# One core of a hybrid decoder layer: stationary expert weights for gate and up, 96 places an expert, buffers for 18 chunks, split distance 4

## The chip, the core and the metric

The kernel runs on one core of a Trainium2 chip. The core has a matrix engine (TensorE, PE in the rows), a vector engine (VectorE, DVE), a scalar engine (ScalarE, ACT), a general engine (GpSimd, POOL) and a queue for transfers (SyncE, SP), each with its own instruction stream, and 16 DMA engines that they share. The metric is the device time of one execution in microseconds (us), lower is better.

## The reference

One decoder layer over 512 tokens of width 1024, in float32. After a block of four token mixers comes a mixture of experts, and the change lies there alone:

```
def hier_moe(x, w_rg, b_rg, w_re, b_re, w_g, w_u, w_d):
    """Top-1 expert group, then top-2 experts inside it; SwiGLU experts."""
    ...
    for e in range(N_EXPERTS):
        h = jax.nn.silu(xt @ w_g[e]) * (xt @ w_u[e])
        out = out + gates[:, e:e + 1] * (h @ w_d[e]).astype(f32)
```

There are 16 experts with hidden width 512, and each of the 512 tokens goes to two of them, so an expert gets 64 tokens on average. `w_g` and `w_u` are 1024 by 512 an expert, `w_d` is 512 by 1024; all three are 100 MB together.

## The kernel before

Up to about 640 us the core computes the mixers. Then it routes: each token gets a place in the buffer of each of its two experts. If every expert has at most `CAP` = 128 tokens (`fits`, true for this input), the routed path runs, else a dense one that is not executed here.

**Chunks and steps.** The weights of an expert are six chunks of 1 MB: `g` 0 and 1, `u` 0 and 1, `d` 0 and 1. The table `STEPS` puts all 96 in one order: g, g, u, u of expert e, then d, d of expert e-1 (at the end: g14, d13, u14, g15, u15, d14, d15, two each). Chunk c is loaded by SP (`stage_load`, L445) into one of `NS` = 8 staging buffers. ACT writes its float16 upper half (`split`, L839), DVE the float16 lower half (`split`, L1726), into one of `NW` = 7 pairs of buffers. Then PE multiplies. A staging buffer is free when DVE has split it, and that lets SP issue the load of chunk c+8; a split buffer is free when PE has used it. ACT and DVE split chunk c+`LOOK` (6 ahead) at step c, before the other work of the step.

**A step on PE.** Every product is made of three (`products`, L963 to L965: upper by upper, upper by lower, lower by upper), each with its own load of the stationary operand. In all steps the tokens' activations are stationary (128 by 128) and the weights move, 512 columns at a time: 12 matmuls a step. Gate and up come out with a token in each row, so `h_transposes` (L1314) must turn the hidden values before the down step can use them.

**The chain of one expert.** POOL gathers its token rows (L566, two buffers `xg`). `x_transposes` on PE (L1306), placed behind u1 of the expert before, `x_hi` on ACT (L893, 2 of 512 columns) and `x_lo` on DVE (L1832, 2 of 512 columns) give `xgT`, held for two experts. After g1 ACT takes the tanh (L906), after u1 DVE makes the gated product (L1901, L1902), PE turns it, ACT and DVE halve it (L914, L1837; `H_AT` says at which steps), and PE uses it in the d steps. ACT copies the result out (L924) and POOL scatters it to rows in memory (L574). The last two experts are put back by matmuls (L1356) instead; the other rows are read back and added on DVE (`add_rows`, L1846, at four steps of `ROWS_AT`).

**Who waits for whom.** All queues run in order, so whatever stands behind a waiting instruction waits too. At u1 DVE does: split, `x_lo` of the next expert, gated product.

## Time and profile before

| | us |
|---|---|
| median of the runs | 971.64 |
| lowest | 970.34 |
| the profiled execution, its own time | 972.64 |
| its span in the trace | 970.7 |

So 1.94 us of the profiled execution lie around its span. The page gives busy time and share of the span:

```profile
PE 907.7 (94%) x5924; PEld 518.1 (53%) x5924; DVE 669.6 (69%) x877; ACT 491.5 (51%) x681; POOL 71.3 (7%) x89
L963 PE MATMUL bank<-arena 128*128 128x512 f16 (+1 forms) x1568 | 466.6, 318 | 16.4 <-DVE arena L1832 6.0
L1726 DVE SCALAR_TENSOR_TENSOR arena<-arena 128x2048 f16<-128x2048 f32 x96 | 217.1, 2286 | 42.6 <-ACT arena L839 42.6
L839 ACT ACTIVATE arena<-arena 128x2048 f16<-128x2048 f32 x96 | 181.5, 1908 | 24.8 <-PE bank L965 24.8
```

A group's row gives the line, the engine and the operation, what is written from what, the shape, the count, the busy time in us and the mean of one in ns, and then the idle time of the engine just before and what ended it. PE's busy time is of overlapping instructions; how long one takes of the engine is read from the distance between starts. PEld is the load of the stationary operand, which can run beside a matmul.

### The profile page before, as it was taken

How to read it: one execution, taken by the hardware profiler on the slowest of the kernel's cores; microseconds unless marked ns; L12 is line 12 of the kernel's file. 1: busy time of each engine (PE TensorE's matmuls, PEld its weight loads, DVE VectorE, ACT ScalarE, POOL GpSimd, SP SyncE). 2: the span in 40 equal slices, each digit the busy share in tenths (PEclk: the TensorE clock that was granted, in tenths of full speed). 3: DMA queues.
4: the chain of work that ended last, by engine and by line, in shares of the span. 5: the costliest groups of instructions: out<-in, count | busy, mean ns of one | idle time of the engine just before them, and what ended most of it. 6: DMA issues, size and time to landing. Idle time of an engine off the chain costs nothing.

```text
span 970.7 us, 14670 instructions
## 1 busy us (share of the span) xinstructions
PE 907.7 (94%) x5924; PEld 518.1 (53%) x5924; DVE 669.6 (69%) x877; ACT 491.5 (51%) x681; POOL 71.3 (7%) x89
## 2 busy tenths in 40 slices
PE   6999999999999998999999979928999999999884
PEld 4434784855766655444444449924455554545442
DVE  5677769541887775643344344557899999999887
ACT  5444373223454444233232324463787888888643
POOL 7000000003000000000000000010111211111000
PEclk9989999999999999999999989957999999999998
DMA  8702404527621102943443316255899999999742
GB/s 211 176 25 59 116 24 111 151 66 198 176 79 33 38 23 65 391 111 94 120 118 83 104 46 234 95 201 170 295 388 403 380 405 391 389 399 379 309 185 89
DMA packets 119454, 177.92 MB, mean 183 GB/s; under 512 B 14317, under 2 KB 99621, under 8 KB 107094
## 3 DMA queue, kind: packets, MB, share of 16 engines
q1 hardware_dynamic: 112176, 162.76, 48.8%
q0 software_dynamic: 6928, 13.61, 4.8%
q8 instruction: 49, 0.80, 0.3%
q10 hardware_dynamic: 278, 0.56, 0.2%
q14 instruction: 23, 0.19, 0.1%
HBM read 172.76 MB, written 16.22 MB: 195 GB/s over the span
## 4 chain that ended last, share of the span: by engine, by line
PE 88%; DVE 6%; ACT 3%; DMA 1%; issue 1%; DVEq 0%; ACTq 0%; POOLq 0%
PE bank L963 25%; PE bank L964 24%; PE bank L965 24%; PE bank L1176 3%; PE bank L1195 3%; PE bank L1306 2%; DVE arena L1726 1%; PE bank L1070 1%; PE bank L1185 1%; PE bank L1055 1%; ACT arena L839 1%; PE bank L1267 1%; PE bank L1314 1%; PE bank L1134 1%; DMA cst<-in_c_sq 1%
## 5 line engine op out<-in xcount | busy, mean ns | idle before, releaser
L963 PE MATMUL bank<-arena 128*128 128x512 f16 (+1 forms) x1568 | 466.6, 318 | 16.4 <-DVE arena L1832 6.0
L964 PE MATMUL bank<-arena 128*128 128x512 f16 (+1 forms) x1568 | 466.3, 318 | 0.0
L965 PE MATMUL bank<-arena 128*128 128x512 f16 (+1 forms) x1568 | 465.4, 317 | 0.0
L1726 DVE SCALAR_TENSOR_TENSOR arena<-arena 128x2048 f16<-128x2048 f32 x96 | 217.1, 2286 | 42.6 <-ACT arena L839 42.6
L963 PEld LDWEIGHTS bank<-arena 128*128 128x128 f16 x1568 | 155.7, 99 | 146.2 <-issue 36.5
L965 PEld LDWEIGHTS bank<-arena 128*128 128x128 f16 x1568 | 155.1, 99 | 112.6 <-issue 5.4
L964 PEld LDWEIGHTS bank<-arena 128*128 128x128 f16 x1568 | 154.9, 99 | 101.0 <-issue 4.9
L839 ACT ACTIVATE arena<-arena 128x2048 f16<-128x2048 f32 x96 | 181.5, 1908 | 24.8 <-PE bank L965 24.8
L606 ACT ACTIVATE arena<-arena 128x1024 f16<-128x1024 f32 (+1 forms) x92 | 92.5, 1007 | 101.9 <-PE bank L965 76.3
L1471 DVE SCALAR_TENSOR_TENSOR arena<-arena 128x1024 f16<-128x1024 f32 (+1 forms) x91 | 103.5, 1163 | 11.4 <-ACT arena L606 9.9
L660 ACT ACTIVATE arena<-bank 128x512 f32<-128x512 f32 x35 | 20.8, 595 | 92.3 <-PE bank L965 92.2
L780 ACT ACTIVATE arena<-arena,nmx 128x128 f32<-128x128 f32 (+3 forms) x48 | 26.9, 561 | 61.4 <-DVE nmx L1671 61.4
L1717 DVE SCALAR_TENSOR_TENSOR arena<-arena,bank 128x512 f32<-128x512 f32 x24 | 16.4, 685 | 57.7 <-PE bank L965 57.6
L830 ACT ACTIVATE arena<-bank,half 128x512 f32<-128x512 f32 x24 | 16.3, 679 | 49.8 <-PE bank L965 49.8
L1668 DVE TENSOR_TENSOR arena<-bank,arena 128x128 f32<-128x128 f32 (+3 forms) x48 | 23.5, 489 | 22.5 <-PE bank L1176 18.8
L1715 DVE SCALAR_TENSOR_TENSOR arena<-arena,bank 128x512 f32<-128x512 f32 x8 | 5.5, 687 | 48.1 <-PE bank L965 48.1
L1176 PE MATMUL bank<-arena 64*128 64x128 f32 (+3 forms) x96 | 38.6, 482 | 0.0
L1195 PE MATMUL bank<-arena 128*128 128x64 f32 x240 | 32.5, 267 | 1.2 <-ACT arena L789 1.1
L1195 PEld LDWEIGHTS bank<-arena 128*128 128x128 f32 x240 | 30.5, 191 | 3.0 <-ACT arena L789 2.2
L893 ACT ACTIVATE arena<-bank 128x512 f16<-128x512 f32 x32 | 17.5, 594 | 22.1 <-PE bank L1306 22.1
L574 POOL DMA_INDIRECT y_rows<-arena,row_of x14 | 21.9, 1561 | 92.1 <-ACT arena L924 92.1
L566 POOL DMA_INDIRECT arena<-x_rows,token_of x16 | 17.7, 1106 | 143.5 <-PE bank L1306 120.3
(275 smaller groups left out, 766.9 us busy)
## 6 DMA issues: line engine op xcount, KB each, us to landing
arena<-in_moe_wg SPq DMA_DIRECT2D x32, 1024.0 KB, 10.3
arena<-in_moe_wu SPq DMA_DIRECT2D x32, 1024.0 KB, 10.8
arena<-in_moe_wd SPq DMA_DIRECT2D x32, 1024.0 KB, 12.1
arena<-in_w_gate SPq DMA_DIRECT2D x32, 512.0 KB, 4.0
arena<-in_w_in SPq DMA_DIRECT2D x31, 512.0 KB, 3.9
arena<-in_w_branch SPq DMA_DIRECT2D x32, 192.0 KB, 3.6
y_rows<-in_c_tab SPq DMA_DIRECT2D x4, 1024.0 KB, 12.3
arena<-in_w_out SPq DMA_DIRECT2D x8, 512.0 KB, 5.0
```

Source lines behind the costliest of these rows:

```text
L574: pool.indirect_dma_start(out=y_rows, out_offset=bass.IndirectOffsetOnAxis(ap=row_of[:, e:e + 1], axis=0), in_=yout[e % 2], in_offset=None ...
L606: act.activation(*split_views(c, c_hi), ACT.Copy, scale=WSCALE).then_inc(S("c_hi_done"), 1)
L780: act.activation(pr[n % 3][:, 0:nk], lg[n % 3][:, 0:nk], ACT.Exp, bias=nmx[:, n % 4:n % 4 + 1], accum_out=lsum[:, (n // HEADS) % 2, n % HE ...
L839: act.activation(w_hi[c % NW], stage[c % NS], ACT.Copy, scale=WSCALE).then_inc(S("hi_done"), 1)
L963: pe.matmul(outb, lhs[0], rhs[0], start=first, stop=False, skip_group_check=True)
L964: pe.matmul(outb, lhs[0], rhs[1], start=False, stop=False, skip_group_check=True)
L965: return pe.matmul(outb, lhs[1], rhs[0], start=False, stop=last_, skip_group_check=True)
L1176: pe.matmul(lgb[n % 2][:, 0:(i + 1) * P], q[r, h // 2, i * P:(i + 1) * P], k[r, h // 2, 0:(i + 1) * P], start=True, stop=True).then_inc(S( ...
L1195: last = pe.matmul(ps[6 + g % 2][:, h * HD:(h + 1) * HD], pT[:, n % 2, b * P:(b + 1) * P], v[:, b, h * HD:(h + 1) * HD], start=(b == 0), s ...
L1471: ins = stt(lo, src, WSCALE, hi, ALU.mult, ALU.subtract)
L1668: sig("lg_read", tt(l, lgb[n % 2][:, 0:nk], bias[:, head, T - nk:T], ALU.add))
L1726: tell("split_done", stt(w_lo[c % NW], stage[c % NS], WSCALE, w_hi[c % NW], ALU.mult, ALU.subtract))
```

## The change

`CAP` falls from 128 to 96, `LOOK` from 6 to 4, the staging buffers go from 8 to 12 and the split pairs from 7 to 6 (together 18 chunks where there were 15). In the gate and up steps the weights become stationary, 128 hidden columns at a time, and the 96 token columns move: 48 matmuls a step. The hidden values then come out already turned, and `h_transposes`, `H_AT` and the buffers `hrow` go. The activations `xgT`, `sgr` and the gathered rows `xg` now have one buffer each where they had two. The d steps keep their 12 matmuls of 512 columns, with 96 stationary columns. Loads of d chunks take two rows of 4 KB for each partition where they took one run of 8 KB.

```
-CAP = P
+CAP = 96
-LOOK = 6
+LOOK = 4
...
+        STAGE = [17408, 24576, 29696, 44172, 46220, 26624, 33292, 35340, 4096, 6144, 10752, 15360]
+        SPLIT = [(40076, 41100), (42124, 43148), (37388, 38412), (0, 1024), (2048, 3072), (28672, 31744)]
+        EARLY, READY = 5, 10
+        SLOT = [*range(READY), *range(FIRST), READY, FIRST, READY + 1]
+        for _c in range(len(SLOT), len(STEPS)):
+            SLOT.append(SLOT[_c - NS])
...
-                for c in range(NS + FIRST, len(STEPS)):
-                    sp_.wait_ge(S("split_done"), c - NS + 1)
+                for c in range(READY + FIRST, len(STEPS)):
+                    if splits_ahead(c):
+                        sp_.wait_ge(S("split_done"), splits_ahead(c))
+                    elif c > READY + FIRST:
+                        sp_.wait_ge(S("x2_stored"), 16 * NT)
+                        sp_.wait_ge(S("token_full"), 2)
                     stage_load(c)
...
                 def x_hi(e):
                     for j in range(2):
                         act.wait_ge(S("xgT_full"), 2 * e + j + 1)
-                        if e >= 2:
-                            act.wait_ge(S("chunk_used"), steps_to("u", e - 2))
+                        if e >= 1:
+                            act.wait_ge(S("chunk_used"), steps_to("u", e - 1))
...
                         for k in range(4):
-                            last = products(bank[:, :], (hi[:, 4 * hf + k, :], lo[:, 4 * hf + k, :]),
-                                            (v[0][:, k, :], v[1][:, k, :]), hf == 0 and k == 0, hf == 1 and k == 3)
+                            for m in range(KH):
+                                last = products(bank[:, m * CAP:(m + 1) * CAP], [w[:, k, m * P:(m + 1) * P] for w in v],
+                                                (hi[:, 4 * hf + k, :], lo[:, 4 * hf + k, :]),
+                                                hf == 0 and k == 0 and m == 0, hf == 1 and k == 3)
...
-                    if (kind, e, hf) in H_AT:
-                        h_lo(H_AT[kind, e, hf])
+                    if STEPS[c - 1][0] == "u" and STEPS[c - 1][2]:
+                        h_lo(STEPS[c - 1][1])
...
-                    if c in ROWS_AT:
-                        add_rows(ROWS_AT[c])
...
+                    if c >= len(STEPS) - NT:
+                        add_rows(c - len(STEPS) + NT)
```

The order of the instructions changes at three places. The first is PE at the start of a g step in the middle of the expert phase; bank2 is the accumulator, and "waits" are the semaphores that the instruction waits for. Before, and then of the change:

```order
L963 MATMUL bank2<-arena 128x512 [waits split_done,h_ready,xlo_done]
L964 MATMUL bank2<-arena 128x512
L965 MATMUL bank2<-arena 128x512
L963 MATMUL bank2<-arena 128x512
L964 MATMUL bank2<-arena 128x512
L965 MATMUL bank2<-arena 128x512
```

```order
L977 MATMUL bank2<-arena 128x96 [waits split_done,h_ready,xlo_done]
L978 MATMUL bank2<-arena 128x96
L979 MATMUL bank2<-arena 128x96
L977 MATMUL bank2<-arena 128x96
L978 MATMUL bank2<-arena 128x96
L979 MATMUL bank2<-arena 128x96
```

The waits are the same; each matmul has 96 columns for 512, and there are 48 in the step for 12. The second place is DVE over the cycle of one expert. L1726 (now L1732) is the split of a chunk, L1832 (L1838) `x_lo`, L1901 and L1902 (L1899, L1900) the gated product, L1837 (L1843) `h_lo`. Before, and then of the change:

```order
L1726 SCALAR_TENSOR_TENSOR arena<-arena 128x2048 [waits hi_done]
L1832 TENSOR_TENSOR arena<-bank,arena 128x512 [waits xhi_done] x2
L1901 SCALAR_TENSOR_TENSOR arena<-arena,bank 128x512 [waits hgT_full,chunk_used,sgr_ready]
L1902 SCALAR_TENSOR_TENSOR arena<-arena,bank 128x512 [waits dve_step_routed]
L1726 SCALAR_TENSOR_TENSOR arena<-arena 128x2048 [waits hi_done] x5
L1837 TENSOR_TENSOR arena<-bank,arena 128x512 [waits hhi_done]
```

```order
L1838 TENSOR_TENSOR arena<-bank,arena 128x384 [waits xhi_done] x2
L1899 SCALAR_TENSOR_TENSOR arena<-arena,bank 128x384 [waits chunk_used,sg_ready]
L1900 SCALAR_TENSOR_TENSOR arena<-arena,bank 128x384 [waits dve_step_body]
L1732 SCALAR_TENSOR_TENSOR arena<-arena 128x2048 [waits hi_done]
L1843 TENSOR_TENSOR arena<-arena 128x384 [waits hhi_done]
L1732 SCALAR_TENSOR_TENSOR arena<-arena 128x2048 [waits hi_done] x5
```

Still six splits and five small operations, but the small ones have 384 columns, and `h_lo` stands one split behind the gated product and no longer five. The third place is DVE at the end, from the gated product of expert 15 on; L1846 (L1848) is `add_rows`, L1851 (L1853) the lower half of a result of the last two experts. Before, and then of the change:

```order
L1837 TENSOR_TENSOR arena<-bank,arena 128x512 [waits hhi_done]
L1846 SCALAR_TENSOR_TENSOR arena<-arena,wsel 128x1024 [waits tokens_in0]
L1846 SCALAR_TENSOR_TENSOR arena<-arena,wsel 128x1024 [waits dve_step_routed]
L1901 SCALAR_TENSOR_TENSOR arena<-arena,bank 128x512 [waits chunk_used,hgT_full,sgr_ready,dve_step_routed]
L1902 SCALAR_TENSOR_TENSOR arena<-arena,bank 128x512 [waits dve_step_routed]
L1846 SCALAR_TENSOR_TENSOR arena<-arena,wsel 128x1024 [waits tokens_in1]
```

```order
L1732 SCALAR_TENSOR_TENSOR arena<-arena 128x2048 [waits hi_done] x3
L1899 SCALAR_TENSOR_TENSOR arena<-arena,bank 128x384 [waits chunk_used,sg_ready]
L1900 SCALAR_TENSOR_TENSOR arena<-arena,bank 128x384 [waits dve_step_body]
L1843 TENSOR_TENSOR arena<-arena 128x384 [waits hhi_done]
L1848 SCALAR_TENSOR_TENSOR arena<-arena,wsel 128x1024 [waits tokens_in0]
L1848 SCALAR_TENSOR_TENSOR arena<-arena,wsel 128x1024 [waits dve_step_body]
```

Because splits now run 4 steps ahead, three of them stand between `h_lo` of expert 14 and the gated product of expert 15, and all four `add_rows` come behind that product, where the first came ahead of it.

## Rows read from the trace of the kernel before

**Rows 1.** Windows: span, PE, PEld, DVE, ACT, POOL busy; granted clock, DMA share, GB/s.

```profile
700.00:908.00 208.00, 208.00 (x1025) 104.16 (x1023) 201.34 (x136) 173.74 (x148) 30.85 (x24) 1.00 1.00 391
908.00:930.00 22.00, 16.97 (x76) 8.03 (x75) 16.17 (x11) 14.82 (x13) 2.16 (x2) 0.92 0.55 201
```

**Rows 2.** Chain that ended last: start, length, what; two x_transposes, 12 experts apart.

```profile
694.62 1.07 PE bank L1306 x8
...
899.50 1.06 PE bank L1306 x8
```

**Rows 3.** Timeline, DVE over one expert: start, length, operation, [idle before].

```profile
696.45 1.28 DVE L1832 TENSOR_TENSOR arena<-bank,arena 128x512 f16<-128x512 f32 x2
697.65 0.68 DVE L1901 SCALAR_TENSOR_TENSOR arena<-arena,bank 128x512 f32<-128x512 f32 x1
698.36 0.69 DVE L1902 SCALAR_TENSOR_TENSOR arena<-arena,bank 128x512 f32<-128x512 f32 x1
698.97 4.49 DVE L1726 SCALAR_TENSOR_TENSOR arena<-arena 128x2048 f16<-128x2048 f32 x2
703.82 4.49 DVE L1726 SCALAR_TENSOR_TENSOR arena<-arena 128x2048 f16<-128x2048 f32 x2 [0.37 <-ACT arena L839]
...
710.72 0.68 DVE L1837 TENSOR_TENSOR arena<-bank,arena 128x512 f16<-128x512 f32 x1
```

**Rows 4.** Timeline, ACT in the same expert.

```profile
701.87 3.71 ACT L839 ACTIVATE arena<-arena 128x2048 f16<-128x2048 f32 x2
...
712.31 1.08 ACT L893 ACTIVATE arena<-bank 128x512 f16<-128x512 f32 x2 [1.20 <-PE bank L1306]
```

**Rows 5.** Timeline, PE: two f16 matmuls of 512 columns, 12 apart.

```profile
780.91 0.38 PE L963 MATMUL bank<-arena 128*128 128x512 f16 x1
...
783.50 0.38 PE L963 MATMUL bank<-arena 128*128 128x512 f16 x1
```

**Rows 6.** Timeline, PE: two f16 matmuls of 128 columns, 20 apart.

```profile
629.91 0.22 PE L963 MATMUL bank<-arena 128*128 128x128 f16 x1
...
631.02 0.22 PE L965 MATMUL bank<-arena 128*128 128x128 f16 x1
```

**Rows 7.** Timeline, PEld: 10 f16 loads from neighbouring columns, before 16-column matmuls.

```profile
646.50 0.34 PEld L1274 LDWEIGHTS bank<-sel,cst 128*128 128x128 f16 x10 [4.15 <-DVE sel L1765]
```

**Rows 8.** Timeline, PE: 64 matmuls of 5 columns, stationary every 16th column.

```profile
668.19 4.07 PE L1293 MATMUL bank<-told,arena 128*128 128x5 f16 x64
```

**Rows 9.** DMA, 700 to 908 us: queue of SP; gathers, count, us to landing.

```profile
q1 hardware_dynamic: 10299, 74.95, 92.0%
...
arena<-x_rows,token_of POOLq DMA_INDIRECT x11, 8.4
```

**Rows 10.** DMA issues, 700 to 750 us: count, KB, us to landing.

```profile
arena<-in_moe_wg SPq DMA_DIRECT2D x6, 1024.0 KB, 7.5
```

**Rows 11.** DMA issues, 850 to 900 us.

```profile
arena<-in_moe_wg SPq DMA_DIRECT2D x6, 1024.0 KB, 14.2
```

**Rows 12.** Timeline, DVE: the last operation of the table of places.

```profile
673.71 0.17 DVE L1865 CAST row_of<-slotv 128x16 uint32<-128x16 f32 x1
```

**Rows 13.** Timeline, PE: the first step of expert 1.

```profile
681.94 0.60 PE L963 MATMUL bank<-arena 128*128 128x512 f16 x1 [2.04 <-DVE arena L1832]
```

**Rows 14.** Timeline, DVE: x_lo of expert 15, an add_rows, lower halves, first sum.

```profile
928.26 1.28 DVE L1832 TENSOR_TENSOR arena<-bank,arena 128x512 f16<-128x512 f32 x2
...
949.52 2.60 DVE L1846 SCALAR_TENSOR_TENSOR arena<-arena,wsel 128x1024 f32<-128x1024 f32 x2
952.24 1.41 DVE L1851 SCALAR_TENSOR_TENSOR arena<-bank,slotw,arena 128x512 f16<-128x512 f32 x2
954.90 2.87 DVE L1908 TENSOR_TENSOR arena<-bank,arena 128x512 f32<-128x512 f32 x4 [1.26 <-PE bank L1356]
```

**Rows 15.** Timeline, ACT: table load behind the last tanh.

```profile
935.60 1.28 ACT L908 ACT_TABLE_LOAD   x1
```

**Rows 16.** Chain that ended last: h_lo of expert 13.

```profile
913.19 0.61 DVE arena L1837
```

More of the change, by code:

```diff
@@ L139 @@
 STEPS[_at:_at + 4] = STEPS[_at + 2:_at + 4] + STEPS[_at:_at + 2]
-H_AT = {}
-for _e in range(NE):
-    if _e == ROUTED - 1:
-        H_AT["g", _e + 1, 1] = _e
-    elif _e == NE - 1:
-        H_AT["d", _e - 1, 1] = _e
-    else:
-        H_AT["u", _e + 1, 0] = _e
 def steps_to(kind, e):
@@ new lines, in build @@
+        w_lo = [arena[:, a:a + CHUNK // 2].bitcast(F16) for _, a in SPLIT]
+        gain2 = arena[:, 48268:48268 + D]
+        onehot = view(XS, NT, CAP * NE // 2).bitcast(F16)
+        onehot_near = view(39436, NT, CAP * NEAR // 2).bitcast(F16).rearrange("p t (c e) -> p t c e", e=NEAR)
+        slots = view(19456, CAP * NE // 2).bitcast(F16)
+        xg = arena[:, 8192:8192 + D]
+        xgT = [view(9216 + 384 * j, KD * CAP // 2).bitcast(F16).rearrange("p (k c) -> p k c", c=CAP) for j in range(2)]
@@ L482, in _ @@
             with sp_.Else():
-                for c in range(NS):
-                    sp_.wait_ge(S(f"stage_landed{c}"), 32 if c < FIRST else 16)
+                for i in range(READY):
+                    sp_.wait_ge(S(f"stage_landed{i}"), 32 if i < FIRST else 16)
                 sp_.wait_ge(S("split_done"), NW)
@@ L551, in _ @@
             with pool.If(fit):
-                for n in range(NE + 2):
+                for n in range(ROUTED + 3):
                     if n == 4:
@@ L1282, in _ @@
                 for t in range(NT):
-                    last = pe.matmul(ps[7][:, 2 * e:2 * e + 2], onehot_near[:, t, :, e], told[:, t, 0:2, e],
+                    last = pe.matmul(ps[7][0:CAP, 2 * e:2 * e + 2], onehot_near[:, t, :, e], told[:, t, 0:2, e],
                                      start=(t == 0), stop=(t == NT - 1))
@@ L1911, in add_last @@
                     sig("moe_done", ins)
-                ending(add_last)
+                ending(add_last, nf)
             with dve.Else():
-                new_chain("dve_step_dense", before)
+                new_chain("dve_step_body", before)
                 for j, w in enumerate((w1, w2)):
```

202 lines of the change are left out of this document (93 added, 109 removed).

## The prediction

> **What bounds the kernel now.** I read the windows first. From 700 to 908 us PE is busy in the whole window at the full granted clock (2.4 GHz), DVE for 201.34 of 208 us, ACT for 174 us, and the DMA share is 1.00 at 391 GB/s [rows 1]. So three resources are near their limits at once, and the trace must say which sets the pace. The chain of waits shows the transposes of two experts, 12 experts apart: (899.50 - 694.62) / 12 = 17.07 us an expert [rows 2]. PE's own work explains it. Two 512-column matmuls, 12 apart, start 2.59 us apart, so one costs 216 ns [rows 5]; 72 of them are 15.5 us, x_transposes add 1.07 us, and the four h_transposes about 0.5 us by the same rate. PE sets 17.07 us. DVE does 201.34 / 12.2 = 16.5 us in that time, only half a microsecond less. The page's 94% for PE says nothing on that.
>
> The DMA engines hide a third limit. SP's queue moved 74.95 MB in 208 us [rows 9], 360 GB/s, so six chunks (6.29 MB) take 17.5 us, a little longer than 17.07. That they fall behind shows in the time from issue to landing, 7.5 us at first and 14.2 us at last [rows 10, 11]. The kernel lives on the chunks loaded ahead.
>
> **The change, part by part.** *PE.* A gate or up step has 48 matmuls of 96 columns for 12 of 512. No row has 96 columns. From above: f16 matmuls of 128 columns, each with its own load, go at 1.11 / 20 = 55.5 ns [rows 6]. With 512 columns at 216 ns this is 0.418 ns a column plus 2 ns, so 96 columns are 42.1 ns, if the load keeps up. From below: ten loads of neighbouring columns took 0.34 us, of which one is about 0.1, so (0.34 - 0.1) / 9 = 27 ns each, and that at the clock of 1.2 GHz [rows 7]. The new stationary operands are neighbouring columns too. 64 matmuls of 5 columns took 4.07 us, 61 to 64 ns each, with every 16th column as the stationary operand [rows 8]; that price is the upper end. I take 42.1 ns, since 27 lies below it and the nearest row, 128 columns, is column-bound. Then the four steps cost 192 x 42.1 ns = 8.1 us for 10.35, the d steps stay at 5.2, x_transposes with 96 columns are 0.8 to 1.07, h_transposes vanish: 14.1 us an expert, 3 us less. PE stops being the bound.
>
> The Trainium skill speaks against this: "TensorE: Matmul & The Clock Gate", section Back-to-back issue gap, says that a sustained stream of load and matmul pairs runs at about 81 ns each with 128 columns. By it the four steps would cost at least 15.6 us and PE 21.6 an expert. By this rule the trace disagrees, since it shows such pairs at 55.5 ns.
>
> *DVE.* Six splits stay, 4.49 us for two, 13.47 in all [rows 3]. The other five operations lose 128 of 512 columns; between the 2048-column split (2.245 us) and the 512-column operation (0.60 us from start to start) a column costs 1.07 ns, so each loses 0.137 us. DVE's work goes from 16.6 us (13.47 + 1.20 + 1.32 + 0.60) to 15.9 us. It is the new bound.
>
> *ACT.* Splits of 1.86 us, small operations at about 0.54 each, 0.43 with 384 columns [rows 4]: 11.1 + 4 x 0.43 + 1.1 = 13.9 us. But `h_hi` now stands one split behind `x_lo`: ACT waits for DVE's gated product (1.05 us after `x_lo`), then does `h_hi` 0.43, split 1.86, result 1.08, split 1.86 = 5.2 us, while DVE has split, `h_lo`, split = 4.95 us. DVE waits 0.3 us. So an expert takes 15.9 + 0.3 = 16.2 us.
>
> *Loads.* At 2.91 us a chunk the DMA engines would need 17.5 us an expert. What covers this is the lead: 17 chunks are issued by the time the table of places is made (673 us), with DVE at chunk 6. The other 79 take 79 x 2.91 = 230 us and land by 905. ACT wants the last at about 920. This cover of 15 us is gone at 3.1 us a chunk, and each 0.1 us more then costs 8 us. The single `xg` is gathered one period ahead in place of two; 16 us cover a gather that lands in 8.4 [rows 9].
>
> *Start.* The chain to the first step loses about 0.5 us with narrower transposes and halves, and gives as much back to chunk 15, which is now on the DMA engines when the first gather starts. The table's one-hot rows shrink from 2048 to 1536 columns and the split behind them goes: about 1 us. I take 672.9 for the end of the table, now 673.9 [rows 12].
>
> **The sum**, from there to the end of `x_lo` of expert 15, on DVE: 86 splits of 2.245 = 193.1; 15 pairs `x_lo` of 0.97 = 14.6; 14 gated products of 1.05 = 14.7; 14 `h_lo` of 0.47 = 6.6; one-hot rows 0.6. That is 229.6. Waits: 12 x 0.3 = 3.6, and at the start 3.7. There PE runs four steps alone after an idle stretch, at the clock of 1.2 GHz, as it does now after 2.04 us of idling [rows 13]: 1.4 us till `x_lo` of expert 1, and 2.3 us for ACT behind g1's tanh. Sum: 672.9 + 229.6 + 7.3 = 909.8. Now this point is at 929.5 [rows 14], so 19.7 us are won. Three of them are the old stall of d13, which waited on `h_lo` of expert 13 [rows 16]; it falls away since that has no transposes now and comes six steps earlier.
>
> *The end* gives some back. After `x_lo` of expert 15 PE has idled about 5 us and starts cold: g15 is 3.9 + 2.0. Then the tanh and its table load (1.28 [rows 15]) with 0.2, at 7.8; ACT's split of chunk 94, at 9.7; on DVE the splits 94 and 95, at 14.2; gated product 15.3; `h_hi` and `h_lo` 16.4; `add_rows` 2.62 at 19.0; lower half 1.33; two `add_rows` 25.6; lower half 26.9; the last `add_rows` 29.5. The first sum stands there. It now comes 954.9 - 929.5 = 25.4 us after `x_lo` [rows 14], so 4.1 us are lost. Behind it nothing changes, 15.8 us to the end of the span.
>
> 909.8 + 29.5 + 15.8 = 955.1 us for a span of 970.7. With the 1.94 us around it the profiled execution would be 957.0 for 972.64; the median is 1 us below that, so the forecast is **956.0 us**, 1.6% less than 971.64. (A measurement of this kernel can tell about 2% from no change.)
>
> **Rivals.**
> *The cover holds better (19%).* PE idles about 2 us before each g step, which I let pass without cost or gain; if ACT's split comes through between and the clock stays up at the end (it was 0.92 of full speed over 908 to 930 us in spite of two stalls [rows 1]), 3.6 us of waits, 2 of the start's and 2 of the end's go: 948 us.
> *Loads bind (11%).* A price of 3.2 us a chunk, for the d rows of 4 KB or the scatters, costs about 8 us: 964. For it speaks the growth to 14.2 us [rows 11]; against it the 15 us of cover.
> *PE binds after all (13%), slower than before.* If 96-column matmuls with a fresh operand went at the 61 ns of rows 8, PE would need 192 x 0.061 + 5.2 + 0.83 = 17.7 us an expert. From 679 us 14 experts are 248, d13 5.2 and a cold start 3 more: 935, plus 29.5, 15.8 and 1 us: 981 us. It decides from 57.6 ns on, where PE is back at 17.07. Against it: those operands are strided, and 27 ns with neighbouring columns. The instruction stream is the other way there: 4 times the matmuls at a DMA share of 1.00. At 81 ns it would be 14 x (21.6 - 17.7) = 55 us more, 1036 us; by the skill's page this is the case. I give all above 991 us 5% of the 13.
> *My forecast (57%)*, 950 to 961.
>
> That the change does not do what it says would show as 512-column matmuls in gate and up; the order rules it out.
>
> **Numbers.** 2% are 952.2 and 991.1 us. Faster than 952.2: the better case (19%) and a tenth of mine and little more, 0.28. Slower: 0.05. Within: 0.67. The range 946 to 970 leaves out the PE case's 13% and some 5% below.
>
> **What the new profile would show.** Right: starts of 96-column matmuls 42 ns apart; x_transposes about 16.2 us apart; DVE near 98% busy from 700 to 890 us, ACT's split ending its waits; PE busy by starts for 14 us and idle ahead of g steps; time to landing above 15 us at last, with no wait of ACT for it. Wrong: PE without idle time and DVE waiting for `x_hi` (PE binds); ACT's split waiting for a transfer after 850 us (loads bind); a first sum more than 31 us behind `x_lo` of expert 15 (the end).

## The result, and the profile after the change

The changed kernel takes 963.93 us (median of 7 runs, 963.55 to 968.07), the kernel before 970.88 in the same session. The ratio is 0.9942, with a 95% interval of 0.9931 to 0.9953. So the change gains 0.6%, where 1.6% was forecast. The ratio is formed over all fast runs (one of the seven executions before the change took 1364.6 us and is a slow one), so it is not the quotient of the two medians, 0.9928. The profiled execution is the longest of the seven: 968.07 us, span 966.3 for the forecast's 955.1.

The windows of the changed kernel (columns as in [rows 1]):

```profile
661.00:677.00 16.00, 16.00 (x136) 16.00 (x134) 2.98 (x4) 4.09 (x3) 0.00 (x0) 0.61 0.04 13
677.00:700.00 23.00, 21.82 (x330) 19.42 (x330) 20.52 (x24) 13.05 (x13) 2.78 (x2) 0.90 0.85 305
700.00:842.00 142.00, 130.83 (x2017) 108.32 (x2015) 139.47 (x99) 119.72 (x107) 37.80 (x19) 1.00 1.02 388
842.00:920.00 78.00, 63.59 (x896) 53.64 (x896) 68.54 (x47) 60.49 (x53) 12.80 (x8) 0.89 0.95 362
```

Three stretches with different limits, and a short restart. From 700 to 842 us it is as forecast: DVE is busy 98% of the time (139.47 of 142) and PE no longer all of it. From 661 to 677 us PE is busy, for the most part with one loop, DVE hardly works and the DMA engines move 13 GB/s. From 842 us DVE falls to 88% and PE to 82%, while the DMA share is still 0.99 to 1.01 up to 900 us; the 0.95 of the whole stretch comes from its last 20 us, when the stream runs out.

DVE's timeline shows the period. These are `x_lo` of experts 2, 12, 13, 14 and 15:

```profile
696.69 1.01 DVE L1838 TENSOR_TENSOR arena<-bank,arena 128x384 f16<-128x384 f32 x2
...
859.04 1.01 DVE L1838 TENSOR_TENSOR arena<-bank,arena 128x384 f16<-128x384 f32 x2
...
876.86 1.02 DVE L1838 TENSOR_TENSOR arena<-bank,arena 128x384 f16<-128x384 f32 x2
...
896.51 1.02 DVE L1838 TENSOR_TENSOR arena<-bank,arena 128x384 f16<-128x384 f32 x2
...
919.50 1.01 DVE L1838 TENSOR_TENSOR arena<-bank,arena 128x384 f16<-128x384 f32 x2
```

From expert 2 to expert 11 (841.42 us) the step is 16.03 us (one of 16.45), where it was 17.07 [rows 2]. Then come 17.6, 17.8, 19.7 and 23.0. The last step would be 20.4 without any wait for weights (shown below), because eight splits stand on DVE between `x_lo` of expert 14 and that of 15, in place of six. So about 9.5 us are lost in these four steps.

**The first loss.** DVE's timeline at the table of places (the row before the change is in [rows 12]), and the timeline of PE that it waits for ([rows 8] before):

```profile
660.42 3.56 DVE L1879 TENSOR_TENSOR arena<-arena,rank 128x1536 f16<-128x1536 f16 x4
677.30 0.16 DVE L1860 COPY slotw<-bank 96x2 f32<-96x2 f32 x1 [13.32 <-PE bank L1307]
...
678.69 0.17 DVE L1867 CAST row_of<-slotv 96x16 uint32<-96x16 f32 x1
```

```profile
665.62 11.64 PE L1307 MATMUL bank<-told,arena 128*96 128x5 f16 x64
```

The same 64 matmuls took 4.07 us with 128 stationary columns and take 11.64 us with 96, 182 ns each in place of 64. (`128*96` in the row is the stationary operand.) Everything up to there came 2 us sooner than before (no more than executions differ: `x_lo` of expert 0 starts between 654.0 and 660.7 us in the runs below), but the table stands at 678.9 us in place of 673.9. While DVE waits it makes no splits, so no weight buffer comes free, and chunk 17 waits for the table itself. That is the pause of the DMA engines in the first window.

**The second loss.** The waits of the changed kernel from 842 to 920 us (engine and line, what it waited for: us in total, times, longest):

```profile
DVE arena L1732 <- ACT arena L850: 9.2, 16, 1.4
ACT arena L850 <- DMA arena<-in_moe_wg: 7.4, 8, 1.7
ACT arena L850 <- DMA arena<-in_moe_wd: 3.6, 6, 1.6
ACT arena L850 <- DMA arena<-in_moe_wu: 2.3, 4, 0.9
```

ACT's half of the split waits 13.3 us for weights, and hands 9.2 us of it on to DVE. The first of these waits ends at 840.1 us, and the kernel before the change has none at all. The DMA issues of 850 to 900 us (count, size, us from issue to landing) beside [rows 11]:

```profile
arena<-in_moe_wd SPq DMA_DIRECT2D x7, 1024.0 KB, 27.9
arena<-in_moe_wu SPq DMA_DIRECT2D x6, 1024.0 KB, 26.2
```

26 to 28 us where it was 14.2. With 12 buffers more loads are in flight, so the landing time alone does not say that they come too late; ACT's waits do.

**As forecast.** PE in a gate step, 30 matmuls apart (the 96-column ones, [rows 5, 6] before):

```profile
682.00 0.21 PE L979 MATMUL bank<-arena 128*128 128x96 f16 x1
```

The one 30 further on starts at 683.28 us, so one costs 42.7 ns at the clock of 2.4 GHz. At 1.2 GHz they are 80 ns apart (660.98, 661.06, 661.14). DVE's rows of the end:

```profile
930.44 4.49 DVE L1732 SCALAR_TENSOR_TENSOR arena<-arena 128x2048 f16<-128x2048 f32 x2 [4.01 <-ACT arena L850]
...
950.23 2.87 DVE L1909 TENSOR_TENSOR arena<-bank,arena 128x512 f32<-128x512 f32 x4
```

### The profile page after: what moved, and what is told of

The parts are those of the page before. It is cut to its first block, busy times and chain, and to the rows that moved or that the text cites. A ratio compares the mean times of both kernels' runs of the same rounds, so it can differ in the third digit from the quotient of the medians.

```text
span 966.3 us, 19139 instructions
## 1 busy us (share of the span) xinstructions
PE 881.2 (91%) x8164; PEld 591.7 (61%) x8164; DVE 657.6 (68%) x877; ACT 481.5 (50%) x681; POOL 85.6 (9%) x89
## 4 chain that ended last, share of the span: by engine, by line
PE 64%; DVE 16%; DMA 9%; ACT 7%; issue 3%; ACTq 0%; DVEq 0%; POOLq 0%
PE bank L977 17%; PE bank L978 16%; PE bank L979 16%; DVE arena L1732 8%; ACT arena L850 4%; PE bank L1190 3%; DMA arena<-in_moe_wd 3%; DMA arena<-in_moe_wu 3%; DMA arena<-in_moe_wg 3%; PE bank L1209 3%; PE bank L1084 1%; PE bank L1199 1%; PE bank L1307 1%; DVE arena L1838 1%; DVE arena L1848 1%
## 5 line engine op out<-in xcount | busy, mean ns | idle before, releaser
L977 PE MATMUL bank<-arena 128*128 128x96 f16 (+3 forms) x2336 | 511.0, 264 | 35.8 <-DVE arena L1838 26.3
L978 PE MATMUL bank<-arena 128*128 128x96 f16 (+3 forms) x2336 | 510.3, 264 | 0.0
L979 PE MATMUL bank<-arena 128*128 128x96 f16 (+3 forms) x2336 | 509.3, 264 | 0.5 <-issue 0.5
L977 PEld LDWEIGHTS bank<-arena 128*128 128x128 f16 (+1 forms) x2336 | 238.5, 102 | 137.8 <-issue 33.4
L979 PEld LDWEIGHTS bank<-arena 128*128 128x128 f16 (+1 forms) x2336 | 237.8, 102 | 78.2 <-issue 3.1
L978 PEld LDWEIGHTS bank<-arena 128*128 128x128 f16 (+1 forms) x2336 | 237.6, 102 | 68.5 <-issue 2.1
L1732 DVE SCALAR_TENSOR_TENSOR arena<-arena 128x2048 f16<-128x2048 f32 x96 | 216.9, 2287 | 39.1 <-ACT arena L850 38.9
L617 ACT ACTIVATE arena<-arena 128x1024 f16<-128x1024 f32 (+1 forms) x92 | 92.5, 1007 | 102.5 <-PE bank L979 79.7
L791 ACT ACTIVATE arena<-arena,nmx 128x128 f32<-128x128 f32 (+3 forms) x48 | 26.9, 561 | 61.4 <-DVE nmx L1677 61.4
L1723 DVE SCALAR_TENSOR_TENSOR arena<-arena,bank 128x512 f32<-128x512 f32 x24 | 16.4, 685 | 57.7 <-PE bank L979 57.6
L585 POOL DMA_INDIRECT y_rows<-arena,row_of x14 | 30.9, 2207 | 122.2 <-ACT arena L937 122.2
L1674 DVE TENSOR_TENSOR arena<-bank,arena 128x128 f32<-128x128 f32 (+3 forms) x48 | 23.5, 489 | 22.5 <-PE bank L1190 18.8
L577 POOL DMA_INDIRECT arena<-x_rows,token_of x16 | 23.9, 1492 | 90.7 <-PE bank L1319 85.3
L1566 DVE MAX8 m<-arena 128x8 f32<-128x256 f32 (+2 forms) x48 | 26.7, 557 | 0.9
## 6 DMA issues: line engine op xcount, KB each, us to landing
arena<-in_moe_wd SPq DMA_DIRECT2D x32, 1024.0 KB, 18.8
```

What stands on the lines that cost most here:

```text
L585: pool.indirect_dma_start(out=y_rows, out_offset=bass.IndirectOffsetOnAxis(ap=row_of[0:CAP, e:e + 1], axis=0), in_=yout[e % 2][0:CAP, :], ...
L617: act.activation(*split_views(c, c_hi), ACT.Copy, scale=WSCALE).then_inc(S("c_hi_done"), 1)
L791: act.activation(pr[n % 3][:, 0:nk], lg[n % 3][:, 0:nk], ACT.Exp, bias=nmx[:, n % 4:n % 4 + 1], accum_out=lsum[:, (n // HEADS) % 2, n % HE ...
L977: pe.matmul(outb, lhs[0], rhs[0], start=first, stop=False, skip_group_check=True)
L978: pe.matmul(outb, lhs[0], rhs[1], start=False, stop=False, skip_group_check=True)
L979: return pe.matmul(outb, lhs[1], rhs[0], start=False, stop=last_, skip_group_check=True)
```

## The experiments

The theory: two causes took the gain. (1) The token table's matmuls got slower with 96 stationary columns, which delays the first experts and the loads. (2) The stream of weights is slower than the 2.91 us a chunk of the forecast, and holds the last four experts. All runs are compared by their ratio to the kernel before, which ran in each session (970.9 to 971.6 us). For orientation: the change alone 0.9942. The traces start the experts up to 6.7 us apart, so where they are compared as a whole it is from `x_lo` of expert 0 on.

| run | us | ratio | 95% interval |
|---|---|---|---|
| wide table | 957.73 | 0.9865 | 0.9843 to 0.9887 |
| loads from chunk 17 halved | 955.74 | 0.9836 | 0.9816 to 0.9856 |
| both | 949.32 | 0.9771 | 0.9755 to 0.9787 |
| six chunks halved | 959.21 | 0.9873 | 0.9856 to 0.9889 |
| d rows of 8 KB | 964.98 | 0.9933 | 0.9910 to 0.9956 |
| lead of 8 chunks | 976.32 | 1.0059 | 1.0040 to 1.0078 |
| neighbouring 96 columns | 961.59 | 0.9902 | 0.9866 to 0.9938 |
| 128 places | 969.46 | 0.9967 | 0.9954 to 0.9981 |
| before, loads halved | 969.96 | 0.9988 | 0.9976 to 1.0001 |
| distance 5 | 965.00 | 0.9924 | 0.9903 to 0.9946 |
| wide, distance 5 | 957.31 | 0.9860 | 0.9843 to 0.9876 |
| wide, split first | 956.72 | 0.9877 | 0.9842 to 0.9911 |
| 4 in flight | 966.45 | 0.9950 | 0.9935 to 0.9964 |
| wide, 4 in flight | 958.38 | 0.9883 | 0.9846 to 0.9921 |
| wide, 3 in flight | 960.89 | 0.9895 | 0.9873 to 0.9918 |
| wide, 6 in flight | 959.79 | 0.9892 | 0.9870 to 0.9915 |

### The table 128 numbers wide

```diff
-        onehot = view(XS, NT, CAP * NE // 2).bitcast(F16)
+        onehot = view(XS, NT, WIDE * NE // 2).bitcast(F16)        # WIDE = 128
...
-    last = pe.matmul(ps[4][0:CAP, 5 * e:5 * e + 5], onehot...
+    last = pe.matmul(ps[4][:, 5 * e:5 * e + 5], onehot...
```

The numbers and views that the table is written from get the same width.

> The changed kernel with the one-hot table 128 numbers wide again, so that the 64 small matmuls of the token table hold 128 stationary columns as before the change; everything else stays at 96 places. Theory A (the 96 strided stationary columns are what made this table dear, 11.6 us where it was 4.1 us): the 64 matmuls take 4 to 5 us, the places stand in the register table about 7 us earlier (672 in place of 678.9 us), the loads start again 7 us earlier, and the time falls by 7 to 12 us, to 952 to 957. Rival B (the table is dear because TensorE's granted clock is at 0.60 there, whatever the width): the 64 matmuls stay at 10 us or more and the time moves by less than 1 us.

Timelines of PE and DVE in this run:

```profile
663.39 4.08 PE L1308 MATMUL bank<-told,arena 128*128 128x5 f16 x64
```

```profile
667.51 0.16 DVE L1861 COPY slotw<-bank 96x2 f32<-96x2 f32 x1 [4.79 <-PE bank L1308]
```

The matmuls are back at 4.08 us, though one-hot rows are dearer (4.63 for 3.56 us).

The clock is no rival. Windows inside the loop of this run, and then of the changed kernel's:

```profile
663.40:665.40 2.00, 2.00 (x37) 2.00 (x35) 0.00 (x0) 1.80 (x2) 0.00 (x0) 1.00 0.04 8
665.40:667.40 2.00, 2.00 (x36) 2.00 (x36) 0.00 (x0) 2.00 (x2) 0.00 (x0) 0.63 0.00 0
```

```profile
665.70:669.50 3.80, 3.80 (x24) 3.80 (x22) 0.00 (x0) 3.68 (x3) 0.00 (x0) 0.81 0.02 4
673.00:677.20 4.20, 4.20 (x26) 4.20 (x27) 0.00 (x0) 0.00 (x0) 0.00 (x0) 0.50 0.00 0
```

The wide form runs as fast at a granted clock of 0.63 as at 1.00, the 96-column form as slowly at 0.81 as at 0.50. (The counts of a window take in matmuls that reach over its edges; the price of one is the loop's time over 64.) From `x_lo` of expert 0 to that of expert 1 it takes 19.9 us for 27.0. The time falls by 6.2 us between the medians, just outside the 7 to 12 of theory A, and by 7.5 us by the ratios. The last four steps are 16.0, 17.3, 19.2 and 23.3 us in this run: the loads hold them again, with 7.3 us. An earlier start moves the loads and their consumer together, so it cannot cure that.

### The loads taken away

```diff
-                sp_.dma_start(stage[c]..., src)
+                n_ = k // 2 if c >= 17 else k
+                sp_.dma_start(stage[c]...[:, 0:n_, :], src[:, 0:n_, :])
```

> The changed kernel with every weight chunk from number 17 on loaded by half only (the rest of the buffer keeps what it held, so the output is another). It takes the transfers away as a limit. Theory A: the step of 16.03 us an expert holds to the last expert, so that the last four steps give back about 9 us and x_lo(15) ends near 911; the table of places still costs its 11.6 us; time 954 to 956. Rival D (the last experts are slower for another reason: a lower clock, or scatters on GpSimd): the last steps stay at 17.6 to 23 us and the time stays near 964.

The waits of ACT for weights are gone, `x_lo` keeps its step of 16.03 us to expert 14 and the last step is 20.44. DVE's `x_lo` of experts 14 and 15:

```profile
888.62 1.02 DVE L1839 TENSOR_TENSOR arena<-bank,arena 128x384 f16<-128x384 f32 x2
...
909.06 1.01 DVE L1839 TENSOR_TENSOR arena<-bank,arena 128x384 f16<-128x384 f32 x2
```

That is 8.2 us less than the changed kernel between the medians and 10 us by the ratios: cause (2) is worth that. Both causes at once, the two edits together:

> The changed kernel with the 128 numbers wide table, and every weight chunk from number 17 on loaded by half only (the buffers keep old rows, so the output is another). Both suspected losses are taken away at once. Theory A (the start and the loads are two causes): 16.03 us an expert to x_lo(14), 20.4 us for the last step, and the table at about 669; 946 to 949. Rival (the two are one loss seen twice, since the late table is why the loads are late): 954 to 956, no better than either alone.

949.3 us. The single gains are 6.2 and 8.2 us between the medians, together 14.4, and the two edits together bring 14.6; by the ratios it is 7.5 and 10.3, together 17.8, and 16.6. In the traces, from `x_lo` of expert 0 to the end of the span, it is 9.7 and 9.4, together 19.1, and 17.7. Within 2 us they add up, so they are two causes and not one seen twice.

### How much is missing in the stream

The same edit for `30 <= c < 36` alone:

> The changed kernel with only six chunks (30 to 35, six in the middle of the stream) loaded by half, all others whole (the six keep some older rows, so the output is another). It takes 3.1 MB, about 8 us of transfer time, out of the stream long before the last experts. Theory A (the stream of loads is one queue of bytes and the last experts wait since it is some 8 to 9 us short): the waits of ScalarE for weights after 848 us vanish nearly as with all loads halved, the time is 955 to 958. Rival G (what holds the last experts is local to them, such as the scatters, the final buffers or the clock): the last steps stay at 17.6 to 23 us, time 963 to 965.

Six half chunks are 3.1 MB, as much as three whole ones, and so 9 us of transfer at 2.99 us a chunk (the expectation said about 8), taken out early in the stream. ACT waits for weights in this run, over the whole of 700 to 930 us:

```profile
ACT arena L851 <- DMA arena<-in_moe_wd: 1.4, 2, 0.7
ACT arena L851 <- DMA arena<-in_moe_wg: 1.3, 2, 1.1
ACT arena L851 <- DMA arena<-in_moe_wu: 0.9, 2, 0.6
```

3.6 us for 13.3. All steps to expert 14 are 16.03 us, only the last is 23.2 for 20.44. Bytes removed long ahead of the waits remove the waits: the stream is one store of lead that runs down, and nothing local to the last experts holds them. That one still loses 2.8 us, and the time is 959.2, a little more than the 958 expected, so more than 9 us of transfer were missing.

Two parts of the change act on the stream, the shorter rows of the down weights and the lead of 12 buffers:

```diff
-   src = src.rearrange("(k p) n -> p k n", k=k) if kind == "d" else src.rearrange("(p k) n -> p k n", k=k)
+   src = src.rearrange("(p k) n -> p k n", k=k)
```

> The changed kernel with the down weights read as before the change, each partition as one run of 8 KB in place of two rows of 4 KB (this pairs rows of the down weights with other hidden values, so the output is another). Rival C (the shorter rows make the transfers slower, and that is why ScalarE waits for weights from 848 us on): a landing from 800 us on gets shorter and the time falls by 5 us or more. Theory A (the queue moves the same bytes at the same 387 GB/s either way, and the late restart is what is missing): within 1 us of the changed kernel.

Within 1 us of the changed kernel. The queue does move more with longer rows, 53.57 MB for 52.55 in 700 to 850 us, which is 2.94 for 2.99 us a chunk, but this gives nothing that the time shows. Over 76 chunks it should have been worth nearly 4 us; why ACT still waits 13.5 us for weights in this run stays open.

```diff
+                    if c - 7 > splits_ahead(c):
+                        sp_.wait_ge(S("split_done"), c - 7)
```

> The changed kernel with its loads held back to 8 chunks ahead of the splits, as before the change, from chunk 15 on (the 12 buffers stay where they are). Theory A (the transfers are short and each chunk that is not on its way during the table of places is missed at the end): chunks 15 and 16 start some 20 us later, the DMA engines stay full afterwards as they were before the change, so 2 x 3 = 6 us are lost: 968 to 971. Rival K (12 buffers bring nothing, as 8 keep the engines full): 963 to 965.

976.3 us, 12 us worse, where 6 were expected. The steps leave 16.03 us already at expert 8 and lie between 16.8 and 19.7 from there to expert 14. So the two chunks that are not sent before the pause do not explain all of it, and the other 6 us are not split further here. With a lead of 8 chunks the change as a whole would have been slower than before.

### What the 96 columns cost, and the stationary weights alone

```diff
-            return (onehot[:, t, :].rearrange("p (c e) -> p c e", e=NE), slots.rearrange("p (c e) -> p c e", e=NE),
-                    rank[:, t, :].unsqueeze(1).to_broadcast([P, CAP, NE]))
+            return (onehot[:, t, :].rearrange("p (e c) -> p e c", e=NE), slots.rearrange("p (e c) -> p e c", e=NE),
+                    rank[:, t, :].unsqueeze(2).to_broadcast([P, NE, CAP]))
...
```

The numbers and the stationary operand of the matmuls are turned with it.

> The changed kernel with the one-hot table turned, so that the 96 stationary columns of one expert are neighbours (VectorE writes it with the rank as a broadcast along the row, which may cost it more or less than the 4.6 us of now). It tells the stride from the width. Theory A1 (only the two together are dear: a stride with less than 128 columns): the 64 matmuls take 4 us or less, 30 to 60 ns each. Theory A2 (a width below 128 alone is dear): they stay at 80 ns or more each, 5 us and up; 278 ns each if the stride plays no part. The total follows: 3 to 7 us less than the changed kernel in the first case, none in the last.

PE's and DVE's timeline of this run:

```profile
667.16 4.88 PE L1307 MATMUL bank<-told,arena 128*96 128x5 f16 x64 [1.55 <-DVE arena L1879]
```

```profile
660.34 6.76 DVE L1879 TENSOR_TENSOR arena<-arena,rank 128x1536 f16<-128x1536 f16 x4
```

That is 76 ns each on the mean, but at two clocks. Windows of the 64 matmuls alone (PE busy, PEld busy, granted clock, DMA share, GB/s); the first four begin ahead of the loop, so their counts are the matmuls started by then:

```profile
667.00:667.20 0.20, 0.04 (x1) 0.05 (x2) 1.00 0.00 0
667.00:667.65 0.65, 0.49 (x11) 0.50 (x11) 1.00 0.00 0
667.00:669.20 2.20, 2.04 (x31) 2.05 (x32) 0.66 0.04 7
667.00:671.20 4.20, 4.04 (x56) 4.05 (x57) 0.59 0.02 4
669.20:671.20 2.00, 2.00 (x28) 2.00 (x28) 0.50 0.00 0
```

At a granted clock of 1.00 ten start in 0.45 us, 45 ns each; at 0.50 (the last row) 25 start in 2.0 us, 80 ns each. So A1 (30 to 60 ns) holds at 1.00 and A2 (80 or more) at 0.50. (The 4.6 us and the 278 ns of the expectation are not the changed kernel's, which are 3.56 us and 182 ns.) Together with [rows 7], ten loads of 128 neighbouring columns at 27 ns each, there are four prices at the granted clock of 0.50: 27 ns for 128 neighbouring columns, 80 for 96 neighbouring, 61 to 64 for 128 with the stride, 182 for 96 with it. The width and the stride each make the matmul dearer, and the two together most.

The turned table costs DVE 3.2 us more to write. With that paid, expert 1's `x_lo` still comes 20.9 us after expert 0's for 27.0, and the trace is 7.0 us shorter from there to its end. Between the medians the gain is 2.3 us and by the ratios 3.9, with an interval that still touches the changed kernel's.

A rule of the Trainium skill bears on the prices: "TensorE: Matmul & The Clock Gate", Weight-path perf modes, says that the fast load of stationary operands is on only with 128 of them in a type other than FP32, and its section LDWEIGHTS puts a plain load at the number of columns over 1.2 ns, an estimate of 80 ns for 96. By the first, the traces agree (27 ns with 128 neighbouring columns, 80 with 96, both at 0.50; 64 and 182 with the stride). By the second, they agree for neighbouring columns at a granted clock of 0.50 (80), not at 1.00 (45), and not with the stride (182).

```diff
-CAP = 96
+CAP = P
-        STAGE = [..., 4096, 6144, 10752, 15360]
+        STAGE = [..., 4096, 6144, 10752]
...
```

> The changed kernel with 128 places an expert in place of 96 (11 weight buffers then, since the tiles are larger): gate and up weights still stand still. Forecast from the rows: PE 192 matmuls of 128 columns at 55.5 ns are 10.7 us, d steps 5.2, transposes 1.07, so 16.9 us an expert; VectorE 16.5 + 0.3. So the step is 16.9 to 17.0 us in place of 16.03, the loads (18 us of bytes an expert) bind later and less, the table costs 4 us again: 959 to 963. Rival H (the stationary weights alone bring it, the 96 places nothing): at or below 958. Rival I (they bring nothing at 128 places): 968 to 971, as before the change.

The window of 700 to 880 us of this run:

```profile
700.00:880.00 180.00, 180.00 (x2415) 151.10 (x2413) 175.70 (x118) 149.43 (x128) 38.53 (x22) 1.00 1.00 394
```

The step is 16.92 us and PE is busy throughout: the forecast of PE's work was right to 0.1 us. But the total is 969.5 us, outside the 959 to 963 expected and inside rival I's 968 to 971, nearly no gain. `x_lo` of expert 15 comes at 919.32 us, 9 before that of [rows 14], and from there to the end it takes 48.9 us for 42.4 before. So rival I has the number and not the reason: with 128 places the change (stationary weights, 11 buffers, distance 4) wins 9 us on the way, of which 4.3 are the last step (22.6 for 26.9 us), and gives 6.5 back at the end. For 96 places the forecast put the give-back at 4.1 us; this expectation left it out.

The kernel before with its loads halved:

```diff
-    sp_.dma_start(stage[c % NS], src)
+    n_ = CHUNK // 2 if c >= 13 else CHUNK
+    sp_.dma_start(stage[c % NS][:, 0:n_], src[:, 0:n_])
```

> The kernel before, with every weight chunk from number 13 on loaded by half only (the buffers keep old values, so the output is another). Theory A (before the change PE set the pace at 17.07 us an expert and the loads were covered): 970 to 971.5, within 1 us of before. Rival L (the transfers already held the kernel before the change, at about 17.5 us an expert): faster by 3 us or more.

`x_lo` of experts 3 and 13 in this run:

```profile
711.78 1.28 DVE L1833 TENSOR_TENSOR arena<-bank,arena 128x512 f16<-128x512 f32 x2
...
882.51 1.28 DVE L1833 TENSOR_TENSOR arena<-bank,arena 128x512 f16<-128x512 f32 x2
```

170.73 / 10 = 17.07 us an expert with half the bytes: PE set them, as the forecast read it, and the loads were covered.

### The pause of the loads, and versions that could be faster

`LOOK = 5` in place of 4, alone and with the wide table:

> The changed kernel with a split distance of 5 in place of 4. The split of chunk 6 then stands ahead of the table of places on VectorE, which waits there for 13 us anyway, and frees one stage buffer some 15 us sooner; ScalarE asks for each chunk 2.7 us sooner. Theory A (the loads bind the last steps, by the sum of their bytes since the restart): one more chunk is in flight during the pause, worth up to 2.9 us, so 961 to 964. Rival E (the distance itself was what held the steady steps): a step falls below 16.03 us and the time goes down by more than 4 us.

> The changed kernel with the 128 numbers wide table and a split distance of 5 together. VectorE idled 4.8 us before the table of places in the run with the wide table; the split of chunk 6 (2.25 us, behind 1.9 us of ScalarE) now lies in that gap, in place of behind it. Theory A: x_lo of expert 1 comes 2 us sooner than with the wide table alone and one more chunk is loaded during the pause, so the time falls by another 2 to 3 us, to 954.5 to 956. Rival F (the distance costs something elsewhere, as the run with distance 5 alone, which did not get faster, may mean): 957 to 959, no better than the wide table alone.

Neither gained; 965.0 us is outside the 961 to 964 of theory A, and 957.3 is rival F's. The early split does take DVE's wait for the table from 13.3 to 10.2 us, and a buffer comes free sooner. But the last four steps with distance 5 are 16.4, 19.6, 17.8 and 22.7. That is 1.5 us less than in the changed kernel, and 0.9 of it is lost again before expert 1. ACT waits 10.4 us for weights with distance 5, where it was 13.3, and 11.1 for 10.8 with the wide table, so that it asks sooner is not shown to be the reason. To leave that out, only the split of chunk 6 was moved:

```diff
-                    if c == 2:
-                        all_slots()
                     if NW <= c + LOOK < len(STEPS):
                         split(c + LOOK)
+                    if c == 2:
+                        all_slots()
```

> The changed kernel with the 128 numbers wide table, distance 4, and on VectorE the split of chunk 6 put ahead of the read-out of the table of places. VectorE idles 4.8 us there. Theory A: 2.25 us of splitting leave the path, less what the later read-out costs (under 1 us), and chunk 18 starts 3 us sooner while ScalarE asks for no chunk sooner: 954.5 to 956.5. Rival (distance 5, which did the same and gained nothing, failed by something other than ScalarE's earlier demand): 957 to 959.

From `x_lo` of expert 0 to that of expert 1 it takes 18.1 us for 19.9 with the wide table alone. This is not the edit's doing: three other runs with the wide table and the split in its old place show 18.1, 18.1 and 18.2 us too (both halved, 6 and 3 in flight), one 19.8. DVE's wait has only moved, as its row of `x_lo` of expert 1 shows:

```profile
672.73 1.04 DVE L1839 TENSOR_TENSOR arena<-bank,arena 128x384 f16<-128x384 f32 x2 [2.52 <-ACT arena L909]
```

ACT's upper half for expert 1 holds it there (and ACT waits for PE's transposes), not DVE's own work. The last steps take 18.3, 18.8 and 23.7 us. The median is the lowest of the whole versions, but its interval holds the wide table's, so no gain is shown.

### Is it the order or the rate of the transfers

In the changed kernel chunk 92 was issued at 890.31 us and landed at 918.2, where ACT waited for it (timelines of SP's queue and of ACT):

```profile
890.31 17.71 SPq L449 DMA_DIRECT2D arena<-in_moe_wd  x4
```

```profile
918.22 1.91 ACT L850 ACTIVATE arena<-arena 128x2048 f16<-128x2048 f32 x1 [0.21 <-DMA arena<-in_moe_wd]
```

The DMA queue of SP from 677 us to there, and to 910 us:

```profile
q1 hardware_dynamic: 14770, 82.13, 88.7%
```

```profile
q1 hardware_dynamic: 14237, 79.92, 89.4%
```

The 76 chunks up to number 92 are 79.7 MB, reached by 910 us, and the whole stream has 82.84. So when chunk 92 landed, 2.4 of the 3.1 MB of the three behind it had been moved as well. If transfers in flight hold each other up, fewer of them would help:

```diff
+                    if c - 4 > READY + FIRST:
+                        sp_.wait_ge(S(f"stage_landed{SLOT[c - 4]}"), landed(c - 4))
```

> The changed kernel where SP, before it issues a chunk, also waits until the one four ahead of it has landed: the same bytes, buffers and splits, but at most 4 loads in flight in place of up to 9. Theory M (loads in flight share the engines, so each lands as late as those behind it): a landing takes 12 us in place of 26, the DMA share stays at 1.00, ScalarE's waits for weights after 842 us (13.3 us) fall to under 5, the last steps shrink, 956 to 960. Rival N (the engines serve in order of issue and the stream is too slow): the same waits at the same places, 963 to 966; or the engines run dry between loads and it gets slower, 968 and more.

The waits of ACT for weights with 4 in flight, 700 to 930 us, and two kinds of issues of 700 to 850 us:

```profile
ACT arena L852 <- DMA arena<-in_moe_wu: 7.0, 7, 2.9
ACT arena L852 <- DMA arena<-in_moe_wg: 5.3, 8, 1.4
ACT arena L852 <- DMA arena<-in_moe_wd: 1.5, 4, 0.8
```

```profile
arena<-in_moe_wg SPq DMA_DIRECT2D x17, 1024.0 KB, 11.9
arena<-in_moe_wu SPq DMA_DIRECT2D x17, 1024.0 KB, 11.7
```

The landing time falls as theory M said, to 12 us, and ACT waits 13.8 us as before. Theory M has fallen: the landing time counts how many loads stand in line, and a chunk comes no sooner with fewer of them. The total, 966.5 us, is not better either, a little above the 963 to 966 of rival N. The rate fell a little: the queue moved 50.99 MB in 700 to 850 us for 52.55, that is 3.09 us a chunk. What makes the lag between moved and landed is not shown. The Trainium skill's page "DMA: Bandwidth & Descriptors", sections Queues, rings and completion order and Why a DMA increments its semaphore by 16 and not by 1, says that a transfer is split over the rings of up to 16 engines, and that its data have landed only when each of them has reported. By it the lag would be the slowest engine's; no run here shows the engines apart.

The same with the wide table, and with 3 and 6 in place of 4:

> The changed kernel with the 128 numbers wide table and at most 4 loads in flight. Theory M: against the wide table alone (957.7) it gains what it gains without it, 950 to 954, near the 949.3 that halved loads gave. Rival N: 957 to 959.

> The changed kernel with the 128 numbers wide table and at most 3 loads in flight. Before the change a landing of 7.5 us at 2.9 us a chunk (about 3 in flight) went with a DMA share of 1.00, so the engines should stay full. Theory M: as good as 4 in flight or up to 1 us better, 950 to 954. Rival N: 957 or more, and slower than with 4 if the engines run dry.

> The changed kernel with the 128 numbers wide table and at most 6 loads in flight. Theory M: a landing takes about 18 us and the gain lies between none and that of 4 in flight, 953 to 956. Rival N: 957 to 959.

All three at 958 to 961 us, none better than the wide table alone, as rival N had it. With 3 in flight the queue moved 50.64 MB.

## Why the prediction was wrong, and where it was right

The forecast of the span was 955.1 us, the profiled one is 966.3. In the terms of the sum:

| term | forecast | measured | difference |
|---|---|---|---|
| end of the table of places | 672.9 | 678.9 | +6.0 |
| from there to the end of `x_lo` of expert 15, loads aside | 236.9 | 232.1 | -4.8 |
| waits for loads in it | 0 | 9.5 | +9.5 |
| to the first sum | 29.5 | 29.7 | +0.2 |
| to the end of the span | 15.8 | 16.1 | +0.3 |

232.1 is taken from the run with halved loads (677.9 to 910.0 us), 9.5 is the changed kernel's 241.6 less that. The differences sum to 11.2.

**Right: what sets the pace.** 42.7 ns for a 96-column matmul (42.1 forecast), DVE as the bound at 98%, a step of 16.03 us (16.2), a wait of 0.28 us for ACT (0.3) in each. "PE binds after all" is out by the 42.7 ns, and with it the 61 and 81 ns.

**Wrong: "The table's one-hot rows shrink ... about 1 us".** The step on the start priced what DVE writes and passed over what PE does with it. The 64 matmuls of [rows 8] keep their number but change their shape from 128 to 96 strided stationary columns, a form without a row. It should have had both bounds like the 96-column matmul of a gate step; the measured price is 182 ns each, 7.6 us more in all. The +6.0 is less than that because this execution started 2.1 us early, while of the 1 us that the forecast took off only half came. [rows 8] stood in the forecast as the upper end for another operation, and was not used for its own.

**Wrong: "2.91 us a chunk ... land by 905".** The rate was read between 700 and 908 us, where the engines are full. From the issue of chunk 17 (677.67 us) to the landing of chunk 92 (918.2) it is 240.5 / 76 = 3.16 us each. Of the 19 us that this adds over 2.91, by an estimate from these windows, the slower stream of 700 to 850 us (2.99) makes 6; the restart, with a DMA share of 0.85 and 305 GB/s from 677 to 700 us, 3 to 4; and the lag between moved and landed bytes about 9. The other side moved too: DVE gets to `x_lo` of expert 15 in 4.8 us less than forecast, and so asks for the weights sooner. By the forecast's numbers chunk 92 landed at 673 + 76 x 2.91 = 894 us and was wanted near 906.5 (ACT splits it 3.3 us ahead of the end of `x_lo` in the run with halved loads), a cover of 12.3. Less 19.3 and 4.8, and with the 1.2 us that chunk 17 starts ahead of the end of the table, it is 10.6 us short, an estimate beside the 9.5 measured. The late table is not in this sum, since it holds back the splits as much as the loads. The forecast did say that the cover is gone at 3.1 us a chunk and that each 0.1 more costs 8 us, and 3.16 is past it. The rate that was set against it was that of a full queue, without its start and its end. Its rival "loads bind" (11%) had 3.2 us a chunk and a price of 8 us, and the halved loads give back 8.2 to 10; its sign, ACT's split waiting for a transfer late in the experts, is what the trace shows. That its 964 us is also the measured time is luck, for it has neither the table nor the shorter sum on DVE in it, and the d rows of 4 KB, named there as a reason, are no cause that the time shows.

**Off in the other direction: the sum on DVE**, 4.8 us too long. The start's waits were 1.9 us in the run with halved loads (1.24, 0.19, 0.47), and 1.0 with both edits, and not 3.7. The splits in a row go at 2.217 us each (13.30 for six) and not 2.245, which is 2.4 us over 86 of them. The rest, about 0.5 us, is not followed further.

So what bounds the steps was right, and two terms failed, the table's matmuls that were put at nothing and the cover of the loads: losses of 6 and 9.5 us missed, and the rest overstated by 5. With both losses removed the chip gives 949.3 us; the number 956 would have been too high for the kernel that it described.

**Right: the end.** 29.7 us from `x_lo` to the first sum (29.5), with the table load of 1.28 us behind the last tanh, and 16.1 to the end.

The version to keep is the changed kernel with the 128 numbers wide table: 957.7 us, 1.35% less than before (interval 1.1 to 1.6%), against 0.6% for the change as made. What remains above 949 is the stream.

## What to carry to other kernels

When a size is changed everywhere by one constant, list every matmul whose shape it changes, the small ones too, and give each a price with two bounds; the dearest here was a loop of 4 us. A cover for loads is to be reckoned from the issue of the first late chunk to the landing of the one that is wanted, with restart and tail, and not with the rate of a full queue. And in this kernel, once the stream was late, more distance, fewer loads in flight and longer rows moved nothing that could be measured; fewer bytes did, and loads held to a lead of 8 chunks, as with 8 buffers, cost 12 us.

## What the runs showed of the hardware

- A 5-column f16 matmul with a fresh stationary operand takes 61 to 64 ns for 128 columns with a stride of 16 elements and 182 ns for 96 with that stride, at a high and at a low granted clock alike. For 96 neighbouring columns it takes 45 ns at a granted clock of 1.00 and 80 ns at 0.50. 128 neighbouring columns were loaded in 27 ns each at 0.50, ahead of 16-column matmuls [rows 7].
- DVE writes the one-hot table 1.9 times slower (6.76 for 3.56 us) where the rank is broadcast along the innermost direction and not along the next one; only this pair of layouts was tried.
- With 3, 4 or 6 loads of 1 MB in flight SP's queue moved 50.6, 51.5 and 52.8 MB in 150 us, and 53.4 without a limit (all with the wide table), at a DMA share of 1.01 to 1.02 in 700 to 850 us throughout. The share does not tell a full queue from a nearly full one, the megabytes do.
- The landing time is no measure of lateness: of the loads issued from 850 to 900 us, 11 to 13 us with 4 in flight and 26 to 28 us without a limit went with the same 13 to 14 us of waiting.
